# A layer-0 mixer stage rewritten as straight-line code with exact widths, and all its projection columns moved to the first stage

## What is computed

```python
h = rmsnorm(x, norm_w[0]); qa, ka, va, iq, ik, iw, za, qb, kb, vb, zb = split(h @ w_in)     # 3140 columns
# rotary on qa, ka, iq, ik (first 16 of 64) and on qb, kb (all 64)
# mixer A: 8 heads of 64, 2 key/value heads; 4 index heads
sc  = sum_h relu(iq_h . ik / 8) * iw_h          # (row, key), keys <= row
sel = top_k(sc, 256)                             # per row
oa  = softmax(qa . ka[sel] / 8) @ va[sel] * silu(za)
# mixer B: retention, 4 heads, keys of 64, values of 128, state carried from tile to tile
ob  = groupnorm(retention(qb, kb, vb)) * gain * silu(zb)
```

## Time and profile before

| what | value |
|---|---|
| median of 3 runs | 4828.14 us (4827.93 to 4829.86) |
| profiled execution, its own time | 4832.2 us |
| its span | 4830.5 us |
| busy: TensorE / VectorE / ScalarE / GpSimd | 3824 / 2539 / 1233 / 555 us |
| mean granted TensorE clock | 0.88 of 2.4 GHz |
| instructions | 53580 |
| bytes read / written | 167.7 / 81.9 MB |

### The profile page before, as it was taken

The page is one execution under the profiler, slowest core; times in us unless marked ns, Lnnn a source line. Parts: engine busy times, 40 slices in busy tenths (PEclk is TensorE's granted clock), DMA queues, the critical chain, the costliest instruction groups (busy, mean ns, idle before and its releaser), DMA issues. The chain is left out here.

```text
span 4830.5 us, 53580 instructions
## 1 busy us (share of the span) xinstructions
PE 3823.8 (79%) x16393; PEld 2247.3 (47%) x16393; DVE 2539.4 (53%) x5398; ACT 1233.3 (26%) x2376; POOL 554.6 (11%) x1329
## 2 busy tenths in 40 slices
PE   7987788888888878888234389798897985698898
PEld 4543445545555455546112144344443444565665
DVE  0007788888888888985216003214042244665664
ACT  3311223232233333334001011111111112343442
POOL 0000000000000000000002000000000000676573
PEclk9998998888899989999567689899898997799899
DMA  5220100100000000000223410111101012222321
GB/s 191 93 75 26 39 20 20 35 20 21 15 10 20 20 20 16 4 20 7 65 65 83 161 57 27 54 38 44 52 26 56 33 47 91 79 84 92 110 79 66
DMA packets 213002, 251.38 MB, mean 52 GB/s; under 512 B 84180, under 2 KB 161149, under 8 KB 210461
## 3 DMA queue, kind: packets, MB, share of 16 engines
q1 hardware_dynamic: 183008, 226.26, 14.5%
q10 hardware_dynamic: 27776, 18.95, 1.2%
q0 software_dynamic: 2048, 4.20, 0.3%
HBM read 167.72 MB, written 81.92 MB: 52 GB/s over the span
## 5 line engine op out<-in xcount | busy, mean ns | idle before, releaser
L667 DVE TENSOR_SCALAR_CACHE_REDUCE above<-isc,small 128x512 bf16<-128x512 f32 (+3 forms) x384 | 591.9, 1541 | 3.7
L514 PE MATMUL PX<-w_b,hT_next 128*128 128x512 f32 x1088 | 533.4, 607 | 37.0 <-DVE rst L640 20.5
L1554 PE MATMUL QB<-hT,w_c 128*128 128x512 f32 (+1 forms) x1280 | 480.0, 529 | 0.0
L530 PE MATMUL PS<-kT,qT 128*128 128x512 f32 x688 | 374.5, 628 | 86.5 <-DVE small L698 77.7
L555 PE MATMUL PO<-vst,ptT 128*128 128x64 f32 x2752 | 382.1, 293 | 53.0 <-ACT ptT L435 53.0
L555 PEld LDWEIGHTS PO<-vst,ptT 128*128 128x128 f32 x2752 | 368.7, 210 | 66.3 <-ACT ptT L435 56.3
L514 PEld LDWEIGHTS PX<-w_b,hT_next 128*128 128x128 f32 x1088 | 210.3, 195 | 310.3 <-issue 310.3
L1554 PEld LDWEIGHTS QB<-hT,w_c 128*128 128x128 f32 x1280 | 220.3, 191 | 218.1 <-issue 218.1
L435 ACT COPY ptT<-PT 128x512 f32<-128x512 f32 x344 | 197.9, 581 | 475.8 <-PE PT L545 475.8
L428 ACT ACTIVATE sm<-sm,small 128x2048 f32<-128x2048 f32 (+3 forms) x128 | 184.8, 1443 | 502.1 <-DVE small L704 502.0
L698 DVE CUSTOM_DVE_ANT_0 sm<-PS,mb 128x512 f32<-128x512 f32 x344 | 235.4, 691 | 123.8 <-DVEq L111 120.6
(11 more groups left out here) (399 smaller groups left out, 5115.3 us busy)
## 6 DMA issues: line engine op xcount, KB each, us to landing
out_c_all<-crow SPq DMA_DIRECT2D x272, 64.0 KB, 1.6
w_c<-in_w_in_c ACTq DMA_DIRECT2D x8, 1544.0 KB, 18.3
out_pr_all<-pr_out SPq DMA_DIRECT2D x17, 546.0 KB, 3.0
pr<-out_pr_all SPq DMA_DIRECT2D x17, 546.0 KB, 3.6
x_rows<-in_x_all SPq DMA_DIRECT2D x17, 512.0 KB, 4.6
out_hT_all<-hT SPq DMA_DIRECT2D x17, 512.0 KB, 5.1
hT_next<-out_hT_all SPq DMA_DIRECT2D x17, 512.0 KB
yab<-out_yab_all SPq DMA_DIRECT2D x17, 512.0 KB, 3.9
```

Of the source, the lines that this page charges most:

```text
L514: ins = pe.matmul(PX[n % 2][:, 0:b - a], hT[:, c, :], w_b[:, c, a - AW:b - AW], start=(c == 0), stop=(c == KD - 1))
L530: pe.matmul(PS[u % 2][:, :], qT[:, h, :], kT[:, c * CH:(c + 1) * CH], start=True, stop=True).then_inc(S["s_ps"], 1)
L667: link(dve.tensor_scalar(junk[:, 0:W], isc[:, 0:W], mid, 0.0, ALU.is_gt, ALU.add, accum_out=cnt))
L1554: ins = pe.matmul(PB[b % 2][:, 0:N], w_c[:, c, b * P:(b + 1) * P], hT[:, c, 0:N], start=(c == 0), stop=(c == KD - 1))
```

## The change

Projection stage: all 3140 weight columns are held (`w_all`), and each tile has two parts, A (cuts 0 to 2) and B (cuts 3 to 6), B four tiles behind A. VectorE makes hT (one operation per four blocks), hT is no longer stored, `x` has three buffers, PSUM six for the products.

Mixer stage: no loops. A list of steps, each with a place (period x 100 + offset), is sorted once, and each engine issues its own steps in that order. Period n holds the attention of tile n, the second half of the search, rank and mask of tile n + 1, the first half of the search of tile n + 2, and the front of tile n + 3; periods run from -3 to 15. Tiles 0 and 1 need no search, since they have at most 256 keys. Widths are exact: (t + 1) x 128. Query heads go in pairs whose keys lie in the two halves of the partitions, as two matmuls of 64 rows, and so do the index heads. `pr` is double buffered and loaded whole. Rotary, decays, gates, the group norm's wide operations and part of the mask go from VectorE to GpSimd. All else keeps its engine.

```diff
-        w_a = sb("w_a", [P, KD, AW])
+        w_all = sb("w_all", [P, KD, ABW])
...
+        def order():
+            for k in range(NT + 1 + LAG):
+                if k <= NT:
+                    yield k, 0
+                if k >= LAG:
+                    yield k - LAG, 1
...
+def widths(t):
+    return [min(CH, (t + 1) * P - c) for c in range(0, (t + 1) * P, CH)]
+def mixers_order():
...
+    for n in range(-3, NT):
+        b = 100.0 * n
+        f = n + 3
+        if f < NT:
+            add(b - 45, "sp", "load", f)
+            add(b + 4, "pool", "rope", f)
+            add(b + 8, "sp", "keep", f)
+            add(b + 9, "pool", "values", f)
+            add(b + 10, "pool", "kdecay", f)
+            add(b + 10, "pe", "turn_q", f)
+            add(b + 11, "pe", "turn_k", f)
+            add(b + 12, "act", "copy_q", f)
+            add(b + 12.5, "pe", "turn_b", f)
+            add(b + 13, "act", "copy_k", f)
+            add(b + 14, "act", "copy_b", f)
+            add(b + 16, "act", "tanh", f)
+            add(b + 18, "pool", "qdecay", f)
+            add(b + 22, "pool", "gates", f)
+            if f >= 2:
+                units = [(c, j) for c in range(len(widths(f))) for j in range(2)]
+                for k, (c, j) in enumerate(units):
+                    p = b + 28 + 52.0 * k / len(units)
+                    add(p, "pe", "index", f, c, j)
+                    add(p + 2, "act", "relu", f, c, j)
+                    add(p + 4, "dve", "weigh", f, c, j)
+                add(b + 88, "dve", "bounds", f)
+            add(b + 85, "pe", "ret_scores", f)
+            add(b + 85.5, "pe", "ret_state", f)
+            add(b + 86, "dve", "ret_mask", f)
+            add(b + 87, "pe", "ret_out", f)
+            add(b + 89, "dve", "ret_update", f)
+            add(b + 89.5, "act", "ret_copy", f)
+            add(b + 91, "dve", "gn_mean", f)
+            add(b + 92, "pool", "gn_centre", f)
+            add(b + 97, "dve", "gn_square", f)
+            add(b + 99, "pool", "gn_gate", f)
+            add(b + 101, "sp", "store_yb", f)
+        s = n + 2
+        if 2 <= s < NT:
+            for k in range(STEPS // 2):
+                search_step(add, b + 5 + 7.5 * k, s, k)
+        s = n + 1
+        if 2 <= s < NT:
+            for k in range(STEPS // 2, STEPS):
+                search_step(add, b + 3 + 6.0 * (k - STEPS // 2), s, k)
+            add(b + 76, "dve", "rank", s)
+            add(b + 77, "pool", "over_mask", s)
+            add(b + 81, "dve", "mask", s)
+        elif 0 <= s < 2:
+            add(b + 76, "pool", "causal", s)
+        t = n
+        if t >= 0:
+            k = len(widths(t))
+            for r in range(4):
+                q = b + 20.0 * r
+                for c in range(k):
+                    add(q + 20.0 * c / k, "pe", "scores", t, r, c)
+                    add(q + 20.0 * (c + 0.7) / k, "dve", "masked", t, r, c)
+                add(q + 20, "dve", "maxima", t, r)
+                add(q + 21, "act", "exp", t, r)
...
+            add(b + 84, "dve", "inverse", t)
+            add(b + 86, "pool", "gate_a", t)
+            add(b + 103, "dve", "out_a", t)
+            add(b + 104, "sp", "store_ya", t)
...
+                for a in range(2):
+                    half = slice(a * HD, (a + 1) * HD)
+                    if u >= 2 - a:
+                        pe.wait_ge(S["masked"], after(2 * (u - 1) + a))
+                    pe.matmul(PS[(2 * u + a) % 3][:, 0:w], qT[half, t % 4, r, :], kT[half, c * CH:c * CH + w],
+                              start=True, stop=True).then_inc(S["scores_ps"], 1)
...
+            def count(s, n):
+                k, W = s % 3, (s + 1) * P
...
+                    dve.wait_ge(S["counted"], nth("count", s, n - 1))
+                link(dve.tensor_scalar(counted[:, 0:W], isc[:, k, 0:W], m, 0.0, ALU.is_gt, ALU.add, accum_out=above_it))
+                link(dve.tensor_scalar(ph, above_it, TOPK - 0.5, halves[:, k, n:n + 1], ALU.is_ge, ALU.mult))
+                dve.scalar_tensor_tensor(m, ph, halves[:, k, n + 1:n + 2], m, ALU.subtract, ALU.add)\
+                   .then_inc(S["counted"], 1)
...
+            def gn_centre(f):
+                cv = gx[:, :].rearrange("p (h d) -> p h d", d=RV)
+                pool.wait_ge(S["gn_summed"], nth("gn_mean", f))
+                link(pool.tensor_scalar(gsum[:, :], gsum[:, :], -1.0 / RV, None, ALU.mult))
+                link(pool.tensor_tensor(cv, cv, gsum[:, :].unsqueeze(2).to_broadcast([P, RH, RV]), ALU.add))
+                pool.tensor_tensor(gq[:, :], gx[:, :], gx[:, :], ALU.mult).then_inc(S["gn_centred"], 1)
```

More of the change, by code:

```diff
@@ L35 @@
 BIG = 1e30
+FAR = 2.0 ** 100
 AH, HD = 8, 64
@@ L187, in _, with norm @@
+            for t, part in ORDER:
+                if part == 0 and 3 <= t + 2 <= NT:
+                    rows(t + 2)
+                store(t, part)
+            for part in range(2):
+                sp.wait_ge(S["pr_stored%d0" % part], after(16 * (NT // 2 + 1)))
+                sp.wait_ge(S["pr_stored%d1" % part], after(16 * (NT // 2)))
         @block.scalar
         def _(act):
-            def norm(t, s, q):
-                act.wait_ge(S["x0_loaded%d" % s], after(16 * (q + 1)))
-                act.wait_ge(S["rstd0_ready"], after(t))
+            def norm(t):
+                act.wait_ge(S["x0_loaded%d" % (t % 3)], after(16 * (t // 3 + 1)))
+                act.wait_ge(S["rstd0_ready"], after(max(t - 1, 0)))
@@ L280, in tile @@
                     .then_inc(S["rstd0_ready"], 1)
-            with pool.Fori(0, NT // 2) as q:
-                for s in range(2):
-                    tile(2 * q + s, s)
-            tile(NT, 0)
-def tiles(eng, front, hand_over, back, ahead=None):
-    def step(t, U, NK, first):
-        front(t, U, NK)
-        if back and not first:
-            back(t, U, NK)
-        if ahead and first:
-            ahead()
-        if hand_over:
-            hand_over(t)
-    step(0, 0, 1, True)
-    for g in range(GROUPS):
-        with eng.Fori(0 if g else 1, GT) as j:
-            step(j + GT * g, j * (g + 1) + units_before(g), g + 1, False)
-    if back:
-        back(NT, units_before(GROUPS), GROUPS, False)
@@ L308, in layer0_mixers, with search_step @@
+def search_step(add, place, s, k):
+    add(place, "dve", "count", s, k)
+def layer0_mixers(nc, io, S):
     ctx = ExitStack()
@@ L352, in layer0_mixers @@
[L352 to L360 removed]
+        isc = sb("isc", [P, 3, SEQ])
@@ L363, in ps @@
+        gsum, gsq, grs, nhalf = [sb("gn%d" % i, [P, RH]) for i in range(4)]
         def ps(name):
@@ L366, in layer0_mixers, with nth @@
         PX = [ps("PX0"), ps("PX1")]
-        PS = [ps("PS0"), ps("PS1")]
+        PS = [ps("PS%d" % k) for k in range(3)]
         PT = [ps("PT0"), ps("PT1")]
-        PO, PR = ps("PO"), ps("PR")
-        block = ctx.enter_context(nc.Block())
+        PO = ps("PO")
+        ORDER, NTH = mixers_order()
+        COLS = {t: widths(t) for t in range(NT)}
+        LAST = {t: len(COLS[t]) - 1 for t in range(NT)}
+        PAIRS = [(t, r) for t in range(NT) for r in range(4)]
+        def nth(name, *which):
+            return after(NTH[(name,) + which])
@@ new lines, in _ @@
+            dve.wait_ge(S["c_loaded"], after(16 * 8))
+            for name, which in ORDER["dve"]:
+                if name == "weigh":
+                    weigh(*which)
+                elif name == "bounds":
+                    bounds(*which)
+                elif name == "count":
+                    count(*which)
+                elif name == "rank":
+                    rank(*which)
+                elif name == "mask":
+                    mask(*which)
+                elif name == "masked":
+                    masked(*which)
+                elif name == "maxima":
+                    maxima(*which)
+                elif name == "inverse":
+                    inverse(*which)
+                elif name == "out_a":
+                    out_a(*which)
+                elif name == "ret_mask":
+                    ret_mask(*which)
+                elif name == "ret_update":
+                    ret_update(*which)
+                elif name == "gn_mean":
+                    gn_mean(*which)
+                else:
+                    gn_square(*which)
```

1084 lines of the change are left out of this document (568 added, 516 removed).

## The result

The changed kernel takes 4871.4 us (median of 4 runs, 4862.1 to 4876.0) against 4828.0 (4824.1 to 4829.9) for the kernel before: 1.0089 times the time, interval 1.0071 to 1.0106. It is slower, by 43 us; 4890 was predicted.

A forecast was written before the change was run, and what follows sets the result against it. VectorE was taken to pace the mixers' search, hiding the B projection. First stage +466 us, mixers 1587 instead of 1988: +65 on 4832, less 4 for the median, 4893, rounded down to 4890; eight-in-ten range 4745 to 5010.

The forecast's parts named there:

- Part 1: Projection stage: projecting all columns there adds 17 tiles of B projection on TensorE, without slack, +466 us.
- Parts 2 and 3: Mixer stage: VectorE's work at exact widths sums to 1240 us; TensorE's 839 at full clock stays off the path except at the ends.
- Part 4: Mixer stage: work moved to GpSimd fits in each period, but its queue order and other waits stall VectorE, 158 us together.
- The centring: Period boundary: VectorE waits at gn_square for GpSimd's centring, 3.2 us in 12 periods, 38 us.
- The hand-over of the rotation: Period boundary: scores queued behind the rotation's turns come late for VectorE, 2 to 9 us per period, 69 us.
- The other waits: Mixer periods: VectorE waits for relu, the inverse and retention, taken as 3 us per period, 39 us over 13.
- The rival in which GpSimd is held up by VectorE: Mixer boundary: shared SBUF interface doubles GpSimd's 12 us chain, +156 us, 5046 at the far end, 4968 at half; chance 0.14.
- Part 5: Mixer ends: head 10 us, prologue 36, 36 and 42, period 0 50, period 15 65, last stores and hand-over 11.
- The faster case: Mixers: early fronts cover the hand-overs, stalls 60 instead of 158 us, ends shorter; 4758 us, range 4740 to 4818; chance 0.28.
- The half-clock case: Mixers: less-busy TensorE falls to half clock and passes VectorE's sum from period 3; 5000 us, 5216 throughout; chance 0.10.
- The signs of being wrong: Search step not 0.76 + width, first stage growth not 466 us, or VectorE idle under 90 or over 250 in periods 1 to 14.

The follow-up runs named there:

- Experiment 5: Kernel before, given the all-column projection stage, with the B projection left out of its looped mixers and projected rows loaded whole; 5247.6 us, ratio 1.0868.
- experiment 1: Changed kernel with the rotation of a tile placed ahead of the previous tile's centring and gating on GpSimd; 4813.4 us, ratio 0.9971.
- experiment 4: Changed kernel with the search counting over whole chunks of 512 columns again instead of exact widths; 4913.5 us, ratio 1.0181.
- experiment 3: Changed kernel with queries zero-padded to 128 rows, so score matmuls are full height and not paired; 4859.2 us, ratio 1.0064.
- experiment 7: On experiment 2: last 380 projection columns of tiles 4 to 15 projected in the mixers again, two score buffers; 4743.8 us, ratio 0.9824.
- experiment 2: On experiment 1: gn_square moved behind the output and one search step, gating and its store behind it; 4782.4 us, ratio 0.9906.
- experiment 10: Changed kernel with the rotation on VectorE instead of GpSimd, at the same place of the list; 4855.5 us, ratio 1.0059.

## Why the prediction was right, and where it was off

**The sign and its reason.** A projection that was hidden was paid for in the open, and the mixers did not give back as much. The first stage grew by 455 us (466 predicted) and the mixers shrank by 423 (401 predicted). Experiment 5 shows the reason that the prediction argued from the profile: of the projection's work in the mixers only 45 us were on the path.

**Part 1, 466 against 455.** The matmuls cost what the earlier trace rows said: 749 us of PE in this stage against 285 is 464. The rest is idle time that the stage no longer has. It was 316.6 - 285.3 = 31.3 us before and is 772.0 - 748.9 = 23.1 now, so 463.6 - 8.2 = 455.4. The prediction gave the idle time no term.

**Parts 2 and 3, the periods.** Compared by the reductions at L795, which end each period (measured terms rounded):

| | predicted | measured |
|---|---|---|
| head, prologue and period 0 | 174 | 141 |
| periods 1 to 12, work | 1005 | 979 |
| periods 1 to 12, VectorE's waits | 143 | 141 |
| periods 13 to 15 | 254 | 296 |
| close | 11 | 9 |
| sum | 1587 | 1565 |

Exact widths and the count's slope held: the count at 2048 columns takes 2339 ns, as in the earlier trace rows, and the whole search took 669 us of VectorE where 679 were summed, the slowed steps of the last section included. VectorE's work in the stage came to 1212 us against 1240; retention and output (52 against 62) and the search are the largest part of the difference. TensorE was off the path in periods 1 to 12, as part 3 said, though its clock was only 0.57 to 0.78 in them.

**Part 4, the waits.** Right in the sum, and in one of its three terms. The centring cost 31 us in periods 1 to 12 (38 predicted), at L795 as named. The hand-over of the rotation was put at 69; experiment 1 took it away and found 37. Part of it stood where the prediction did not look: the index weighing stands earlier in VectorE's order in periods 1 to 3 and waits for the same rotation, by way of ScalarE's relu. The other waits were put at 36 for twelve periods; they were 23 for the retention's rows, 13 for the inverse and the 36 for relu and scores that experiment 1 left, 72 in all. One term was 32 us too high and another 36 too low. That the sum came out at 141 against 143 is luck.

The rival in which GpSimd is held up by VectorE fell: its two-input operations took 1.26 us at 512 columns, below the 1.33 estimated. It is VectorE that is held up (last section).

The Trainium skill, GPSIMD Engine Reference, section 1, names contention between GpSimd and VectorE instructions with two SBUF inputs. The trace agrees that there is some (a VectorE step of 0.22 us took up to 1.32 beside GpSimd's work, last section), but not on the engine that the prediction had put at risk.

**Part 5, the ends, is the step that failed.** Head and first period took 34 us instead of 46, the next two 27 and 31 instead of 36 and 42, in the change's favour. The last three took 42 us more than 254: 113, 97 and 85 against 106, 83 and 65.

*Period 15* (20 us). The prediction took the pace of the last attention from the earlier trace rows, 2.19 us per unit, 70 for 32 units, took off up to 14 because two matmuls of 64 rows run together, and put 9 on for the last chain. The pace of one unit leaves out the gaps: in the kernel before, the whole of it took 83.8 us, as this window shows.

```profile
2210.50:2294.30 83.80, 74.25 (x448) 54.10 (x448) 28.84 (x101) 36.82 (x51) 0.00 (x0) 0.95 0.03 9
```

It also shows a clock of 0.95, and the sum had no term for another: in the changed kernel the same 448 records ran at 0.78, in 84.7 us, and in experiments 1 and 4, where the clock was 0.95 here, in 70.6 and 71.2. So, by estimate, 14 us of the 20 are the clock. The pairs do run together: one of 512 columns takes about 0.95 us at full clock, against 0.857 for each single matmul in the earlier trace rows. But they give the period far less than 14 us: with full-height scores (experiment 3) it took 73.8 us at clock 1.00, some 3 more than with pairs at 0.95. Why it is shorter than the 83.8 of before even so, no run shows. Over periods 14 and 15 the clock was lower with pairs in every run (experiment 3), so the term that was taken off for them had a cost beside it that was put at nothing.

*Periods 13 and 14* (7 and 14 us). Waits of VectorE, 2146 to 2244 us, and the output that ends period 13:

```profile
DVE ya L767 <- PE PO L557: 22.9, 2, 12.7
DVE sm L743 <- PE PS L534: 11.9, 6, 4.5
```

```profile
2146.32 0.69 DVE L767 TENSOR_TENSOR ya<-PO,ga 128x512 f32<-128x512 f32 x1 [10.16 <-PE PO L557]
```

The first of the two waits at `ya`, 10.2 us, ends period 13, and the second, 12.7, ends period 14. TensorE sets the pace of both ends: the output waits for the last chain of exponentials, turns and values. In period 13 VectorE waited 13.0 us (10.2 here, 2.8 elsewhere) where 3 were taken, and its own time was 100 against 103. In period 14 it waited 26.3 (with 1.7 for the inverse) where 12 were taken, and its own time was 71, as summed. The clock is no full account of it: at 0.84 in experiment 3 period 14 was only 2 us shorter.

**The rivals.** The faster case asked for waits under 93 us in all; they were 141 in twelve periods alone. The half-clock case (5000 us) fell where it mattered: TensorE ran at 0.57 to 0.78 in periods 1 to 12 and VectorE was still later. In periods 14 and 15 TensorE was the later one, at 0.75 and 0.78.

**The signs of being wrong.** VectorE's idle time in periods 1 to 14 was 180 us (141, 13 and 26), inside 90 to 250, and the search step came out as summed. The first stage grew by 455 and not 466. None of the three signs watched period 15, where the largest miss was.

**The noise of the comparison.** The trace pair shows +30 us, the medians +43. The 13 us between them lie in the runs of the changed kernel (4862 to 4876), of which only the fastest was profiled; their place isn't known.

## What to carry to other kernels

Work that one engine does while another sets the pace is nearly free, and a change that collects it in a stage of its own pays its full price: look at what the bounding engine does beside it, not at the busy time removed. Nearly: moved back, such work cost 26 us of the 60 it gave (experiment 7). In an order written by hand, an operation moved to another engine must be placed by when its result is needed at the end of the longest chain behind it, here ahead of the centring and the gating of the tile before; that was worth 58 us, and the next wait on the same boundary 31 more (experiments 1 and 2). When a stage becomes thinner, read the durations of its units together with the clock under which they were taken, and take the length of the whole stretch, not the pace of one unit. Equal sums do not prove equal terms: here two waits were missed by 32 and 36 us in opposite ways.

## What the runs showed of the hardware

**GpSimd slows VectorE's smallest steps.** The search's last step, one column with two inputs in SBUF, took 220 ns before (mean of 384) and 305 after (mean of 336). Groups by line and shape, of the kernel before and of the changed one:

```profile
L669 DVE SCALAR_TENSOR_TENSOR small<-small,halves 128x1 f32<-128x1 f32 x384 | 84.3, 220 | 13.4
```

```profile
L704 DVE SCALAR_TENSOR_TENSOR mid<-fin,halves,mid 128x1 f32<-128x1 f32 x336 | 102.4, 305 | 11.8
```

The mean hides two kinds. With GpSimd idle it takes 0.22 us (256 of the 336). Of the 80 beside an operation of GpSimd 56 took longer, up to 1.32 us, and 53 of these ended within 20 ns of the end of a GpSimd operation with two inputs:

```profile
1372.50 0.93 DVE L704 SCALAR_TENSOR_TENSOR mid<-fin,halves,mid 128x1 f32<-128x1 f32 x1
...
1378.93 0.95 DVE L704 SCALAR_TENSOR_TENSOR mid<-fin,halves,mid 128x1 f32<-128x1 f32 x1
...
1381.50 0.22 DVE L704 SCALAR_TENSOR_TENSOR mid<-fin,halves,mid 128x1 f32<-128x1 f32 x1
```

The first ends at 1373.43, when the gating's product (1372.16, 1.26 long) has ended at 1373.42; the second at 1379.88, when the rotation's last (1378.61, 1.26) has ended at 1379.87. It costs 85 ns x 336 = 29 us. In experiment 10, where the rotation is not on GpSimd, the mean is 264 ns and 27 steps are long.

**On GpSimd a float32 operation with one input wasn't cheaper than one with two.** The gates' 512 columns with a scalar take 1505 ns, a two-input product of as many 1262; the prediction had put these one-input operations at about half of that each (3.9 us for the four of the gates; they took 5.6). It isn't so of every one-input operation: the mask's, in bf16, takes 1902 ns at 2048 columns (L908). Groups by line and shape, POOL, mixers of the changed kernel:

```profile
L879 POOL TENSOR_SCALAR ga<-ga 128x512 f32<-128x512 f32 x16 | 24.1, 1505 | 0.0
L854 POOL TENSOR_TENSOR pr<-rt_a,rt_b 128x512 f32<-128x512 f32 x16 | 20.2, 1262 | 1.3
```

**The low clock sits in one period or the next.** In experiment 1, periods 14 and 15 do the work of the changed kernel's, and the clock is shared out otherwise:

```profile
2095.00:2200.00 105.00, 88.68 (x426) 66.98 (x425) 69.34 (x132) 32.67 (x48) 3.10 (x3) 0.65 0.01 3
2200.30:2270.80 70.50, 65.82 (x448) 49.69 (x448) 23.28 (x75) 33.91 (x48) 1.19 (x2) 0.95 0.01 5
```

104.9 and 70.6 us there, 97.2 and 84.7 in the changed kernel: a single period at the end of such a stage tells little, the two together (175 and 182) more. Their mean clock was 0.77 in both, against 0.84 to 0.91 in the three kernels with full-height scores (experiment 3).

The Trainium skill, TensorE: Matmul & The Clock Gate, part 3, says that matmuls on different rows of the array run concurrently. The trace agrees: where both score buffers are free, the two of a pair start 6 to 8 ns apart. By that rule alone period 15 would have become shorter than before. At the clock of before (0.95) it did, in experiment 1: 70.6 us against 83.8, though with full-height scores at 1.00 it took 73.8 too. At the clock that it was granted in the changed kernel (0.78) it took 84.7.
